# Linear-attention scores in other banks, one masking operation a head, and later places for three pieces of TensorE work

## What is computed

```python
# gated linear attention, 4 heads, chunks of 64 tokens
scores = jnp.where(causal, jnp.einsum('bnhcd,bnhsd->bnhcs', q_dec, k_inv), 0.0)
o_intra = jnp.einsum('bnhcs,bnhsv->bnhcv', scores, vc)
state_inc = jnp.einsum('bnhcd,bnhcv->bnhdv', k_end, vc)
o = o_intra + jnp.einsum('bnhcd,bnhdv->bnhcv', q_dec, s_prev)
# two softmax attentions, 4 heads each, in blocks of 128 queries
#   MLA (dense causal) and DSA (256 or fewer keys chosen by an indexer)
return jnp.concatenate([o_gla, o_dsa, o_mla], axis=-1) @ w_out
```

## Time and profile before

| | us |
|---|---|
| median of 3 runs | 1276.22 |
| lowest, highest | 1275.58, 1276.27 |
| the profiled execution, its time | 1279.59 |
| the profiled execution, its span (first to last instruction) | 1277.9 |
| PE busy in it | 1244.7 |
| DVE, ACT, POOL busy | 772.3, 539.6, 236.7 |
| mean granted TensorE clock | 0.995 |

### The profile page before, as it was taken

One profiled execution on the slowest core, in us unless ns is written; L12 is line 12 of the kernel. 1 busy time (PEld: TensorE's weight loads), 2 busy tenths in 40 slices (PEclk: granted clock), 3 DMA queues, 4 the chain that ended last, 5 costly groups with the idle time before them and its releaser, 6 DMA issues.

```text
span 1277.9 us, 19073 instructions
## 1 busy us (share of the span) xinstructions
PE 1244.7 (97%) x5924; PEld 970.1 (76%) x5924; DVE 772.3 (60%) x1248; ACT 539.6 (42%) x871; POOL 236.7 (19%) x151
## 2 busy tenths in 40 slices
PE   6999998999999999999999999999999999999997
PEld 5766775588888888888886668756888888888886
DVE  5689876644554544544756888685445445545458
ACT  5574336744313223234436643486442232331334
POOL 1123340021120110210521324200201102102016
PEclk9999998999999999999999999999999999999999
DMA  6211220023333222223222212101232222232323
GB/s 225 86 64 50 83 83 2 2 99 112 99 98 98 99 86 95 99 98 98 98 85 83 67 51 83 67 2 33 91 120 99 98 90 100 90 98 98 99 98 131
DMA packets 30447, 110.46 MB, mean 86 GB/s; under 512 B 3504, under 2 KB 3504, under 8 KB 30384
## 3 DMA queue, kind: packets, MB, share of 16 engines
q1 hardware_dynamic: 29088, 103.82, 24.5%
q0 software_dynamic: 864, 4.81, 1.0%
q10 hardware_dynamic: 432, 1.07, 0.3%
HBM read 107.59 MB, written 2.10 MB: 86 GB/s over the span
## 4 chain that ended last, share of the span: by engine, by line
PE 90%; DVE 3%; ACT 3%; issue 2%; DMA 1%; DVEq 0%; ACTq 0%; POOL 0%; POOLq 0%
PE bank L846 18%; PE bank L847 18%; PE bank L845 18%; PE bank L482 6%; PE bank L483 6%; PE bank L484 6%; PE bank L516 2%; PE bank L504 2%; PE bank L503 2%; PE bank L505 2%; PE bank L728 2%; PE bank L755 1%; PE bank L740 1%; DMA x<-in_x 1%; PE bank L542 1%
## 5 line engine op out<-in xcount | busy, mean ns | idle before, releaser
L900 ACT ACTIVATE wh<-raw 128x1024 fp32r<-128x1024 f32 x194 | 204.8, 1055 | 377.2 <-PE bank L847 239.0
L1204 DVE TENSOR_TENSOR wl<-raw,wh 128x1024 fp32r<-128x1024 f32 x158 | 247.2, 1565 | 74.9 <-ACT wh L900 74.9
L845 PE MATMUL bank<-hh,wl 128*128 128x512 f32 x512 | 200.0, 391 | 0.0
L845 PE MATMUL bank<-xmh,wl 128*128 128x512 f32 x512 | 199.3, 389 | 0.0
L847 PE MATMUL bank<-hl,wh 128*128 128x512 f32 x512 | 199.2, 389 | 0.0
L846 PE MATMUL bank<-xmh,wh 128*128 128x512 f32 x512 | 199.2, 389 | 0.0
L847 PE MATMUL bank<-xml,wh 128*128 128x512 f32 x512 | 199.2, 389 | 0.0
L846 PE MATMUL bank<-hh,wh 128*128 128x512 f32 x512 | 199.2, 389 | 0.0
L450 POOL TENSOR_TENSOR x<-x,rsb 128x512 f32<-128x512 f32 x64 | 84.6, 1322 | 580.2 <-DVE rsb L1621 580.2
L482 PE MATMUL bank<-xgh,wl 128*128 128x512 f32 x368 | 150.3, 408 | 11.9 <-DVE xgl L1212 11.5
L1610 DVE TENSOR_TENSOR sqb<-tf 128x512 f32<-128x512 f32 x64 | 44.3, 693 | 181.3 <-ACT hh L1175 181.3
(11 more groups left out here) (196 smaller groups left out, 1680.5 us busy)
## 6 DMA issues: line engine op xcount, KB each, us to landing
raw<-in_stream SPq DMA_DIRECT2D x194, 512.0 KB, 3.3
out_y<-x SPq DMA_DIRECT2D x8, 256.0 KB, 4.3
par<-in_params POOLq DMA_DIRECT2D x2, 916.0 KB, 4.9
x<-in_x ACTq DMA_DIRECT2D x2, 512.0 KB, 7.6
x<-in_x POOLq DMA_DIRECT2D x2, 512.0 KB, 9.7
con<-in_consts POOLq DMA_DIRECT2D x1, 944.5 KB, 4.8
par<-in_params POOLq DMA_DIRECT2D x1, 896.0 KB, 6.5
par<-in_params ACTq DMA_DIRECT2D x1, 20.0 KB, 2.5
```

The source lines that it names most:

```text
L845: pe.matmul(B.t[s][:], wl[:, s, n_block(k)], src_h[:, k], start=(k == 0), stop=False)
L900: act.activation(wh[:, s], raw[:, s], ACT.Copy).then_inc(hi_ready.sem, 1)
L1204: vec.tensor_tensor(wl[:, s], raw[:, s], wh[:, s], ALU.subtract).then_inc(lo_ready.sem, 1)
```

## The change

1. The first pair of scores, `gs0` and `gs1`, moves from banks 2 and 3 to banks 0 and 1. All later names of TURNING shift in their banks.
2. `masked_scores` is one operation a head, 128 partitions by 512 elements, in place of two of 64 by 256. The mask constant is 64 columns wider and holds the zeros of the other half, so POOL's clearing of `sct` (L435) and DVE's wait for it go.
3. The second pair's scores move from step 2 to step 5, the second pair's outputs from step 6 to step 7, with `gst2`, `gst3` and their gates.
4. ACT copies the first two blocks of linear values (`gvt`, L1098) ahead of its last weight unit, not behind it.
5. On DVE, `weighted(4)` stands between the two decay scans, not behind both.
6. `aost0` to `aost2` are summed by PE ahead of that step's `weigh_pair`.
7. Block 1 of the output projection has three products, not two, ahead of the last product of block 0.

```diff
-C_CAUSAL = C_GM + CHUNK
+C_CAUSAL = C_GM + P
...
-SCORE_SLOT = {2: 1}
-OUT_SLOT = {1: 0, 6: 1}
+SCORE_SLOT = {5: 1}
+OUT_SLOT = {1: 0, 7: 1}
...
-TURNING = ["gs0", "gs1"] + [f"lg{j}" for j in range(LEAD)]
+TURNING = [f"lg{j}" for j in range(LEAD)]
...
-    + [(name, (2, 3, 6)[i % 3]) for i, name in enumerate(TURNING)]
+    + [("gs0", 0), ("gs1", 1)] + [(name, (2, 3, 6)[i % 3]) for i, name in enumerate(TURNING)]
...
-                    if u == 11:
-                        pool.wait_ge(*rel_used.at(l, 3 * IDX_H - 1))
-                        alone(pool)
-                        pool.memset(sct[:], 0.0).then_inc(zeroed.sem, 1)
...
+                    if j % PAIR == LAG + 3 and j > PAIR:
+                        b = j // PAIR - 1
+                        stat(l, f"aost{b}", blk, sq_of(f"aost{b}"))
                     if j in OUT_SLOT:
                         gla_out(OUT_SLOT[j])
                     if j >= LAG and (j - LAG) % 2 == 1:
                         weigh_pair(j - LAG - 1)
                     if j % 2 == 0 and N_MLA <= j + PAIR_LEAD < N_ATT:
                         logits_pair(j + PAIR_LEAD)
-                    if j % PAIR == LAG + 3 and j > PAIR:
-                        b = j // PAIR - 1
-                        stat(l, f"aost{b}", blk, sq_of(f"aost{b}"))
...
-                first_out(1, 0, 2)
+                first_out(1, 0, 3)
                 first_out(0, KB - 1, KB)
-                first_out(1, 2, KB)
+                first_out(1, 3, KB)
...
-                    if u == 23:
+                    if u == 22:
                         for tb in range(2):
                             act.wait_ge(*B.filled(l, f"gv{tb}"))
...
-                        weighted(4)
+                            if pr == 0:
+                                weighted(4)
...
-                    for hp in range(2):
-                        r = slice(64 * hp, 64 * hp + 64)
-                        m = con[r, C_GM:C_GM + CHUNK].unsqueeze(1).to_broadcast([64, TB, CHUNK])
-                        op = vec.tensor_tensor(sct[r, h % 2, :, r], src[r], m, ALU.mult)
-                    op.then_inc(*B.on_read(f"gs{h}"))
+                    m = con[:, C_GM:C_GM + P].rearrange("p (a c) -> p a c", a=2)
+                    vec.tensor_tensor(sct[:, h % 2].rearrange("p t (a c) -> p t a c", a=2),
+                                      src.unsqueeze(2).to_broadcast([P, TB, 2, CHUNK]),
+                                      m.unsqueeze(1).to_broadcast([P, TB, 2, CHUNK]), ALU.mult)\
+                        .then_inc(*B.on_read(f"gs{h}"))
...
-                vec.wait_ge(*zeroed.at(l, 1))
```

More of the change, by code:

```diff
@@ L319, in build_trunk @@
         ones_ready = S("ones_ready", 0)
-        zeroed = S("zeroed", 4)
+        zeroed = S("zeroed", 3)
         ik_ready = S("ik_ready", 4)
@@ L1087, in tasks @@
                     if u == 22:
-                        act.wait_ge(*zeroed.at(l, 3))
+                        act.wait_ge(*zeroed.at(l, 2))
                         for pr in range(2):
@@ L1738, in constant_block @@
     c[:, C_EPS] = EPS
-    c[:, C_GM:C_GM + CHUNK] = (i[:, None] % CHUNK) <= np.arange(CHUNK)[None, :]
+    c[:, C_GM:C_GM + P] = ((i[:, None] % CHUNK) <= (i[None, :] % CHUNK)) & (i[:, None] // CHUNK == i[None, :] // CHUNK)
     c[:, C_CAUSAL + T - P:C_CAUSAL + T] = np.where(i[None, :] <= i[:, None], 0.0, NEG)
```

## The result

The changed kernel takes 1282.41 us (median of 6 runs, 1281.72 to 1284.48), the kernel before 1276.24 us in the same session (6 runs, 1275.58 to 1279.14). The ratio is 1.0044, with a 95% interval from 1.0034 to 1.0054: the change costs 6.2 us. The forecast was 1268.3 us, with a range up to 1274.2, so it had the wrong sign and the range missed the time. The profiled execution after took 1284.36 us (before 1279.59), with a span of 1282.7 us (before 1277.9).

What follows compares the result with a forecast made beforehand. PE, busy 97% of the span, was taken as the bound. Terms of 1.94 us a layer (3.9 for two) plus the clock's 4.0 gave 7.9 us off the 1276.22 median: 1268.3 us, range 1266.2 to 1274.2.

Steps and rivals of the forecast that it cites:

- The decay scans: Projections: `weighted(4)` between the scans frees Relu 19 and removes PE's 1.00 us wait; 0.45 us a layer gained, bounds 0 and 1.00.
- The clock: Attention stages: low-clock stretches stand behind idle time the change removes; 3.99 us gained in both layers together, bounds 0 and 5.2.
- my second rival: Clock falls at another point in each run, so the median holds little of the 3.99 us; 1272.3 us, chance 0.16.
- my first rival: Attention stage: the clock drops anew in each layer at the `lg16` wait, losing about 1.4 us a layer; 1271.1, chance 0.20.
- The start of the stage: Attention stage's start: shorter masks and no bank wait for `lg2` let DVE reach the states 0.83 us earlier a layer.
- The second pair: Attention steps 2 to 7: `gst0` loses its 1.67 us wait, two waits of about 0.65 come; net 0.37 us a layer.
- The dense stretch: Attention steps 10 to 15: DVE's new order loses 0.40 us a layer; the `lg16` wait of 1.4 us costs nothing at full clock.
- My third rival: DVE and ACT bound it all the same, absorbing the earlier start and the 0.45 us; 1274.8 us, chance 0.11.
- The end of the stage: Output block 0's last product: one product moved ahead fills 0.69 of its 0.75 us wait; 0.69 us a layer gained.

Runs made afterwards that it cites:

- the third experiment: Changed kernel with one added wait: POOL's subtraction of weight unit 10 waits until both decay scans are done; 1274.92 us, ratio 0.9980 against the kernel before.
- the kernel with the tail alone: Kernel before with only the last three products of output block 0 behind three instead of two of output block 1; 1276.28 us, ratio 0.9993.
- the start alone: Kernel before with only new banks for the first scores and later TURNING names, one mask operation a head, earlier `gvt` copies; 1278.19 us, ratio 1.0007.
- the new banks: Changed kernel with `weighted(4)` put back behind both scans and the tail logits' banks rotated to 3, 6, 2, 7; 1273.27 us, ratio 0.9958.

## Why the prediction was wrong

**The decay scans (+0.45 us a layer; measured -1.95, and up to 3.3 more with the low clock).** This is the step that gave the wrong sign. I walked the chain of the scan, `rel`, `tf` and the square with the durations of the earlier trace rows and wrote that the second scan "ends 2.3 us later, at about 73.2". It ended at 76.1. I had set each duration as the old trace had it, though DVE's operation was moved by 2.6 us into a time at which POOL now runs a subtraction of its own (0.6 us of the 76.1 are the later start of the program, 2.0 are DVE's standing still). POOL's old timeline alone would not have warned me: there the subtraction starts at 72.72, after the moved operation's end. I had written that Relu 19 comes 1.5 us earlier, and did not follow that on: it frees ACT's rounding and with it POOL's subtraction, both 1.56 us earlier, and that brings the two together. I gave the term the bounds "0 ... and 1.00", with no loss in them, though nothing in the rows excluded one. The trace fits a rule of the Trainium skill here ("SBUF — State Buffer", Who interferes with whom): a DVE instruction with two SBUF inputs contends with a GpSimd (POOL) instruction that reads SBUF, and the one that issues second waits until the first has finished. Here POOL's began at 71.76, DVE's at 72.18, and it took 2.67 us where 0.69 was due; by the rule, an estimate of 74.31 - 72.18 + 0.69 = 2.8. And the third experiment shows that even without the collision the term is 0: the 1.00 us comes back as 1.10 in front of `dqst0`. My lower bound was the right value for that part.

**The clock (+4.0 us; 0.5 us in the median that I started from).** Two faults. The first is arithmetic. The profiled execution was 3.37 us above the median of the runs; the low clock of that profile was worth 3.99. Those are largely the same microseconds. I took the drops out of the profile (1279.59 to 1271.7, with the 3.9 of the other terms) and then subtracted the 3.37 once more. The undisturbed profile of the kernel with the tail alone, 1274.48, shows it: with the tail's 1.2 us added back, the kernel before at full clock is at 1275.7, and its fastest run is 1275.58. Between that and the median of 1276.24 lie 0.5 us, and that was all that could be won of it. In the two later sessions it would have been more, 1.8 and 1.2 us (medians 1277.49 and 1276.85), still less than half of what I took. It is what my second rival said (drops not where the runs pay); I gave it 0.16, since I took the narrow spread of three runs for evidence against it. In 55 executions of the kernel before beside the experiments the time went from 1275.57 to 1281.12, and with it went the clock: the 15 with a mean granted clock of 0.999 took 1275.57 to 1276.31 us, the 13 with 0.996 or 0.995 took 1278.14 to 1281.12. The second fault: "all of it stands behind idle time that this change removes". The low stretch also came at waits that the change puts in (`dqst0`, `lg16`), and stayed away in a profile where the old wait of 1.67 us was still there. That was my first rival, and it too came true, in layer 1: 73.05 us for the stage against 71.96 without the drop, 1.1 us, where I had said 1.4. In the changed kernel all six runs had a mean granted clock of 0.994 to 0.996. (A small slip beside it: the 6.9 us of low time do not follow from the mean clock in the earlier trace rows, which gives 7 x 0.47 x 2 = 6.6; finer stretches of the trace do give 6.8.)

**The start of the stage (+0.83 us a layer).** Right as far as it went. The mask operation took 0.68 us, two of them 1.28 (I said 1.31); `lg1` and `lg2` wait no longer. The first of the states stands 3.61 us behind the first scores (189.27 - 185.66), before 4.34: 0.73 us kept, 0.83 predicted. It would be some 0.4 us more without another meeting of DVE with POOL, which also lengthens the wait of step 0's transposes (1.10 us, 0.8 predicted). In the changed kernel, DVE and POOL:

```profile
186.44 1.28 DVE L1474 TENSOR_TENSOR sct<-bank,con 128x512 f32<-128x512 f32 x2
...
188.68 0.67 DVE L1534 TENSOR_SCALAR pb<-pb,rinv 128x128 f32<-128x128 f32 x1
189.27 0.28 DVE L1552 COPY st<-bank 128x128 f32<-128x128 f32 x1
...
186.90 2.37 POOL L430 TENSOR_TENSOR wl<-raw,wh 128x1024 fp32r<-128x1024 f32 x1 [2.96 <-ACT wh L896]
```

The masks, which take a bank of PSUM and one operand of SBUF, run beside POOL as fast as without it (1.28 us for two at 206.27 as well, where POOL is idle); the product from SBUF to SBUF (L1534) ends just behind POOL, which ends at 189.27 (0.67 us; 0.29 at the same place of a later step, and 0.28 before, where POOL was done). No run moves POOL there, so this one is read from the coincidence alone.

**The second pair (+0.37).** The waits came as walked: 0.72 before the scores of step 5 and 0.74 before `lg10` (0.65 predicted for each), 1.56 before `lg16` (1.4), `gst0` 13.31 us after the first scores (13.5), without a wait.

**The dense stretch (-0.40; measured about -0.9, of which -0.40 is the bank of `lg16`).** Start, second pair and dense stretch together were to give 0.80 us a layer. At full clock the stage with all edits but the scan takes 71.97 us, and the old stage with the new tail 72.27: 0.30. Since the waits ahead of it were right to 0.1 us each, the missing 0.5 is the dense stretch's. I counted the operations that the new order puts between two masks, but said of the wait for `lg16` that DVE's work covers it: "nothing, at full clock". That step failed: with `lg16` and the logits behind it in other banks the stage takes 71.57 us, so the old banks and the wait that they bring cost 0.40 us a layer, and without it the three terms give 0.70 of the 0.80. The size of the wait was right (1.56 us, 1.4 predicted), its price was not. My third rival, that DVE and ACT bound the stretch all the same, holds in part: 1.63 us at `lg16` gave 0.40 at the end. I gave it 0.11.

**The end of the stage (+0.69).** Right: 0.70 us of wait between the two orders, 0.62 us a layer in time. I expected the wait to fall to 0.06, and it was 0.38: the whole stage in front of it had moved, and the old order would have waited 1.08 there, not 0.75.

**At the program's start** the changed kernel was 0.6 us later at the first column sum. It is no part of the change: the kernel with the scan alone, whose constants are the old ones, shows 24.37 too, and the one with the new mask constant 23.74.

With sizes as measured, without the scan: start, pair and dense stretch 0.30, tail 0.62, times two, 1.8 us; from an undisturbed 1275.7, 1273.9, beside 1274.91 measured in the median and 1274.19 in its fastest run. With the scan: the five runs at 0.999 of the kernel with the scan put back took about 1274.7, the collision adds 3.9, 1278.6, and the rest of the changed kernel's 1282.41, some 3.8 us, I put down to the low clock of its runs (an estimate from the medians).

## What to carry to other kernels

When an instruction moves, lay the other engines' timelines over its new place before its old duration is used, and move them first by what the change itself releases: here a wait taken from ACT brought POOL 1.56 us forward. A DVE operation with two SBUF operands that started 0.42 us behind a POOL operation which reads SBUF waited until that one ended, and that turned a harmless swap into 2 us a layer. Take low-clock time out of the profiled time or out of the difference to the median, not out of both; the fastest run, and each run's granted clock, are a good sign of what the undisturbed kernel takes. And what is won at a stage's start has to pass what stands behind it: of 1.20 us expected from start and second pair, 0.30 came through at the end of the stage, and 0.70 once a single logit had a bank that was free earlier.

## What the runs showed of the hardware that I had not expected

The overlap of DVE and POOL costs DVE the whole rest of POOL's instruction, not a share: 2.67 and 2.68 us instead of 0.69. It is in this kernel's MLP as well, where POOL's sums meet DVE's subtractions: those of `wl` (L1200) take 1.22 us alone and 2.08 beside POOL's 1.29. DVE and then POOL, after the change:

```profile
429.21 1.22 DVE L1200 TENSOR_TENSOR wl<-raw,wh 128x1024 fp32r<-128x1024 f32 x1
...
432.98 2.08 DVE L1200 TENSOR_TENSOR wl<-raw,wh 128x1024 fp32r<-128x1024 f32 x1 [0.38 <-ACT wh L896]
...
432.68 1.29 POOL L446 TENSOR_TENSOR x<-x,rsb 128x512 f32<-128x512 f32 x1 [47.79 <-DVE rsb L1617]
```

PE is busy without a gap there, so it costs nothing now. And the granted clock of one kernel differs from run to run: PE's idle 3.0 us in front of `dqst0` was followed by full clock in layer 0 and by 1.2 GHz in layer 1 of the same execution (the scan's move alone), and the 1.67 us in front of `gst0` by 1.2 GHz in layer 0 of the kernel before and by full clock in both layers of the kernel with the tail alone. What decides between them, no run here shows; how often it happens differs by kernel (8 of 10 runs low with the start alone, none of 19 with the new banks).
